# Strassen rounds of the last projection: weight sums by accumulating transfers, activation sums in two parts

## What is computed

```python
def _mla_layer(x, qpos, kn, kr, v, kpos, g_norm, w_in, g_qa, w_uq, g_qn, g_qr, w_out):
    ...
    o = _sweep_queries(_mla_block, (qn, qr), qpos, (kn, kr, v, kpos))
    o = o.reshape(B, T, MLA_WIDTH) * jax.nn.silu(gate)
    return x + o @ w_out
```

## Time and profile before

| | |
|---|---|
| median of 3 runs | 2152.32 us (2151.77 to 2152.51) |
| the profiled execution | 2152.91 us, its span 2151.1 us |
| PE | 2140.8 us busy |
| DVE | 1206.8 us busy |
| ACT | 985.7 us busy |
| POOL | 247.8 us busy |
| DMA | 225.31 MB in the span, mean 105 GB/s |
| granted PE clock | 1.0 of full speed |

### The profile page before, as it was taken

The page is one execution under the profiler, slowest core; times in us unless marked ns, Lnnn a source line. Parts: engine busy times, 40 slices in busy tenths (PEclk is TensorE's granted clock), DMA queues, the critical chain, the costliest instruction groups (busy, mean ns, idle before and its releaser), DMA issues.

```text
span 2151.1 us, 33839 instructions
## 1 busy us (share of the span) xinstructions
PE 2140.8 (100%) x11705; PEld 1881.4 (87%) x11705; DVE 1206.8 (56%) x2777; ACT 985.7 (46%) x2287; POOL 247.8 (12%) x261
## 2 busy tenths in 40 slices
PE   9999999999999999999999999999999999999999
PEld 7888888888888888888888988888899999998899
DVE  6645554445554455556223344444467777775986
ACT  5544444434444444444223333443366666665432
POOL 1000000000000000000000000421342001022011
PEclk9999999999999999999999999999999999999999
DMA  5333333333233333333442332343332212223351
GB/s 185 107 104 108 107 102 92 114 108 95 89 112 105 104 104 104 96 115 103 144 143 76 118 103 89 126 134 123 129 103 81 58 49 64 57 60 101 140 173 63
DMA packets 127463, 225.31 MB, mean 105 GB/s; under 512 B 21104, under 2 KB 75120, under 8 KB 127264
## 3 DMA queue, kind: packets, MB, share of 16 engines
q1 hardware_dynamic: 127392, 224.36, 32.9%
HBM read 191.42 MB, written 32.89 MB: 104 GB/s over the span
## 4 chain that ended last, share of the span: by engine, by line
PE 94%; DVE 3%; ACT 1%; issue 1%; DMA 1%; POOL 0%; SPq 0%; DVEq 0%; ACTq 0%; POOLq 0%
PE bank L212 66%; PE bank L2649 8%; PE bank L2001 4%; PE bank L84 1%; PE bank L958 1%; PE bank L934 1%; PE bank L2706 1%; PE bank L2684 1%; PE bank L950 1%; PE bank L2700 1%; PE bank L2686 1%; PE bank L1994 1%; PE bank L926 1%; PE bank L2678 1%; DVE h_tlo L1879 0%
## 5 line engine op out<-in xcount | busy, mean ns | idle before, releaser
L212 PE MATMUL bank<-b_whi,x_hi 128*128 128x512 f32 x1016 | 401.2, 395 | 0.6 <-DVE b_wlo L195 0.6
L212 PE MATMUL bank<-b_whi,x_lo 128*128 128x512 f32 x1016 | 396.8, 391 | 0.0
L212 PE MATMUL bank<-b_wlo,x_hi 128*128 128x512 f32 x1016 | 396.7, 390 | 0.0
L195 DVE SCALAR_TENSOR_TENSOR b_wlo<-b_raw,first,b_whi 128x512 fp32r<-128x512 f32 x254 | 179.2, 746 | 141.3 <-ACT b_whi L182 140.7
L182 ACT ACTIVATE b_whi<-b_raw,first 128x512 fp32r<-128x512 f32 x254 | 169.2, 714 | 158.1 <-PE bank L212 133.1
L212 PEld LDWEIGHTS bank<-b_whi,x_lo 128*128 128x128 f32 x1016 | 190.7, 188 | 40.7
L212 PEld LDWEIGHTS bank<-b_whi,x_hi 128*128 128x128 f32 x1016 | 191.0, 188 | 37.0 <-DVE b_wlo L195 1.3
L212 PEld LDWEIGHTS bank<-b_wlo,x_hi 128*128 128x128 f32 x1016 | 191.0, 188 | 35.4
L212 PE MATMUL bank<-m_whi,x_hi 128*128 128x512 f32 x320 | 125.0, 391 | 0.0
L212 PE MATMUL bank<-m_wlo,x_hi 128*128 128x512 f32 x320 | 124.6, 389 | 0.0
L212 PE MATMUL bank<-m_whi,x_lo 128*128 128x512 f32 x320 | 124.6, 389 | 0.0
(11 more groups left out here) (549 smaller groups left out, 5377.0 us busy)
## 6 DMA issues: line engine op xcount, KB each, us to landing
b_raw<-w_fox SPq DMA_DIRECT2D x127, 512.0 KB, 3.5
m_raw<-w_mla SPq DMA_DIRECT2D x40, 512.0 KB, 3.5
c_raw<-w_out SPq DMA_DIRECT2D x32, 512.0 KB, 3.5
h_ring<-w_out2s SPq DMA_DIRECT2D x16, 768.0 KB, 6.2
f_raw<-w_ukv SPq DMA_DIRECT2D x16, 512.0 KB, 3.6
queries<-e_q SPq DMA_DIRECT2D x16, 480.0 KB, 3.9
e_raw<-w_uq SPq DMA_DIRECT2D x32, 192.0 KB, 2.6
f_qa<-queries SPq DMA_DIRECT2D x16, 320.0 KB, 3.6
```

The lines of the kernel that those rows point to most:

```text
L195: op = eng.scalar_tensor_tensor(lo[:, k, :], raw[:, k, :], self.gain[:, K:K + 1], hi32[:, k, :], ALU.mult, ALU.subtract)
L212: op = eng.matmul(out, a, w[:, k, :], start=(first and k == 0 and i == 0), stop=(last and k == self.kk - 1 and i == len(pairs) - 1))
```

## The change

The weight sums are no longer made by DVE. POOL issues transfers that add a block in memory onto the block in the ring (`accum_op=ALU.add`), by halves (`grow`): B11 + B12 for P5, + B22 for P6, + B21 for P4, all in the slot of B11, and B22 + B12 for P7. Only B11, B22 and B21 are loaded plainly. As only additions are made, signs change in the activation sums, in `take`, in `join` and in the sample rows. `hi` waits for `grown` once for each half. The activation sums are made for seven of the eight units at the pairs (4, 4), (5, 1), (5, 3), (5, 4), and for the eighth at (7, 0).

```diff
--- before.py
+++ after.py
@@ -1665,11 +1665,13 @@
 
     N, ROUNDS, UNITS, SLOTS = 384, 2, 4, 4
     ORDER = ["P1", "P5", "P6", "P3", "P7", "P2", "P4"]
-    ROLE = {"P1": 0, "P5": 0, "P6": 0, "P3": 2, "P7": 1, "P2": 2, "P4": 0}
-    FORMED = {"P5": 0, "P6": 1, "P7": 2, "P4": 3}
-    FORM_AFTER = {"P1": 0, "P5": 1, "P6": 2, "P2": 3}
+    ROLE = {"P1": 0, "P5": 0, "P6": 0, "P4": 0, "P3": 1, "P7": 1, "P2": 2}
+    LOADED = (0, 2, 3)
+    GROWN = {"P5": (0, 1, "P1"), "P6": (0, 2, "P5"), "P7": (1, 1, "P3"), "P4": (0, 3, "P6")}
     PAIRS = ((5, 6), (1, 2), (3, 4))
     ADDS = {"P1": ((0, 0),), "P5": ((1, 1), (0, 1)), "P6": (None,), "P3": ((0, 1),), "P7": (None,), "P2": ((0, 0),),
             "P4": ((1, 0),)}
@@ -1689,7 +1691,8 @@
         self.shi, self.ring, self.thi, self.tlo, self.R, self.tmp, self.resid, self.out = sums_hi, ring, thi, tlo, R, tmp, resid, out
         s, n = c.sem, len(self.ORDER)
         self.in_ = [[s(f"h_in{i}{h}", 1, 16) for h in range(2)] for i in range(3)]
-        self.t_hi, self.t_lo, self.formed = s("h_t_hi", 4 * n), s("h_t_lo", 4 * n), s("h_formed", 16)
+        self.t_hi, self.t_lo = s("h_t_hi", 4 * n), s("h_t_lo", 4 * n)
+        self.grown = [[s(f"h_grown{i}{h}", (3, 1)[i], 16) for h in range(2)] for i in range(2)]
         self.used, self.done = s("h_used", 3 * n), s("h_done", 2 * n)
         self.summed, self.s_hi, self.s_lo = s("h_summed"), s("h_s_hi"), s("h_s_lo")
         self.taken = s("h_taken", 2 * sum(len(a) for a in self.ADDS.values()))
@@ -1722,16 +1725,15 @@
         return self.ring[self.slot(r, self.ROLE[p])][:, 2 * u:2 * u + 2, :]
     def arrived(self, eng, r, role, u):
-        n = {0: 0, 1: 1, 2: 2, 3: 2}[role]
-        i = self.slot(r, n)
-        loads = [(q, role_) for q in range(self.ROUNDS) for role_ in range(4) if self.slot(q, min(role_, 2)) == i]
+        i = self.slot(r, role)
+        loads = [(q, x) for q in range(self.ROUNDS) for x in range(3) if self.slot(q, x) == i]
         self.in_[i][u // 2].wait(eng, 0, loads.index((r, role)) + 1)
     def load(self, sp, r, role, h):
-        i = self.slot(r, min(role, 2))
-        sp.dma_start(self.ring[i][:, 4 * h:4 * h + 4, :], self.w[r, role, h]).then_inc(self.in_[i][h].sem, 16)
+        i = self.slot(r, role)
+        sp.dma_start(self.ring[i][:, 4 * h:4 * h + 4, :], self.w[r, self.LOADED[role], h]).then_inc(self.in_[i][h].sem, 16)
     PIECES = [(0, 0), (1, 1), (0, 1), (1, 0)]
     READY = {(0, 0): "P2", (1, 1): "P7", (0, 1): "P3", (1, 0): "P4"}
@@ -1762,10 +1764,6 @@
             self.load_res(sp, 0, i)
         for r in range(self.ROUNDS):
             more = r + 1 < self.ROUNDS
-            for h in range(2):
-                self.formed.wait(sp, r, 8 + 2 * h + 2)
-                self.wait_split(sp, r, "P3", 2 * h + 1)
-                self.load(sp, r, 3, h)
             self.wait_taken(sp, r, "P3")
             self.store(sp, r, 2)
             if more:
@@ -1778,7 +1776,6 @@
             self.store(sp, r, 5)
             if more:
                 for h in range(2):
-                    self.formed.wait(sp, r, 12 + 2 * h + 2)
                     self.wait_split(sp, r, "P2", 2 * h + 1)
                     self.load(sp, r + 1, 1, h)
             self.wait_taken(sp, r, "P2")
@@ -1805,45 +1802,48 @@
 
-    def form(self, pool, r, j, u):
-        k = slice(2 * u, 2 * u + 2)
-        a, b, c = (self.ring[self.slot(r, i)][:, k, :] for i in range(3))
-        p, dst, x, y, role = (("P1", a, b, a, 1), ("P5", a, c, a, 2), (None, b, c, b, None), ("P6", a, c, a, 3))[j]
-        if p:
-            self.wait_split(pool, r, p, u)
-        if j == 2:
-            self.formed.wait(pool, r, u + 1)
-        if role is not None:
-            self.arrived(pool, r, role, u)
-        pool.tensor_tensor(dst, x, y, ALU.subtract).then_inc(self.formed.sem, 1)
+    def grow(self, pool, r, p):
+        role, k, before = self.GROWN[p]
+        block = {"P5": 1, "P6": 2, "P7": 1, "P4": 3}[p]
+        x = self.ring[self.slot(r, role)]
+        for h in range(2):
+            self.wait_split(pool, r, before, 2 * h + 1)
+            pool.dma_start(x[:, 4 * h:4 * h + 4, :], self.w[r, block, h], accum_op=ALU.add).then_inc(self.grown[role][h].sem, 16)
     def join(self, pool, r, p):
         self.wait_taken(pool, r, p)
         for a, n in {"P6": ((0, 1),), "P7": ((1, 1), (1, 0))}[p]:
             self.wait_res(pool, r, (a, n))
             x = self.R[:, 2 * a:2 * a + 2, n * self.N:(n + 1) * self.N]
-            pool.tensor_tensor(x, x, self.both[:], ALU.add).then_inc(self.joined.sem, 1)
+            pool.tensor_tensor(x, x, self.both[:], ALU.subtract if n else ALU.add).then_inc(self.joined.sem, 1)
     def pool(self, pool):
         for r in range(self.ROUNDS):
+            for p in ("P5", "P6", "P7"):
+                self.grow(pool, r, p)
             self.join(pool, r, "P6")
+            self.grow(pool, r, "P4")
             self.join(pool, r, "P7")
 
-    def add_up(self, eng, i):
-        a11, a12, a21, a22 = (self.view(self.o, k, q) for q in range(2) for k in range(2))
-        dst, x, y, op = ((a22, a21, a22, ALU.add), (a21, a11, a21, ALU.subtract), (a11, a22, a11, ALU.subtract),
-                         (a12, a12, a11, ALU.subtract))[i]
+    def add_up(self, dve, i, part):
+        a11, a12, a21, a22 = (self.view(self.o, k, q)[:, part, :] for q in range(2) for k in range(2))
+        n = (0 if part.start == 0 else 4) + i
         if i:
-            self.summed.wait(eng, 0, i)
-        eng.tensor_tensor(dst, x, y, op).then_inc(self.summed.sem, 1)
+            self.summed.wait(dve, 0, n)
+        if i < 2:
+            op = dve.tensor_tensor(*((a22, a22, a21, ALU.subtract) if i == 0 else (a21, a11, a21, ALU.subtract)))
+        else:
+            x, y = (a11, a22) if i == 2 else (a12, a11)
+            op = dve.scalar_tensor_tensor(x, y if i == 2 else x, -1.0, x if i == 2 else y, ALU.mult, ALU.subtract)
+        op.then_inc(self.summed.sem, 1)
     SPLIT_SUMS = ["P5", "P6", "P3", "P7"]
     def sum_hi(self, act_, p):
         if p == "P5":
-            self.summed.wait(act_, 0, 4)
+            self.summed.wait(act_, 0, 8)
         if p == "P3":
             self.home.wait(act_, 0, 2)
         act_.activation(self.shi[p], self.view(self.o, *self.SUM_AT[p]), ACT.Copy).then_inc(self.s_hi.sem, 1)
@@ -1867,10 +1867,11 @@
                 self.done.wait(eng, r, 2 * j + 2)
     def hi(self, act_, r, p, u):
-        if p in self.FORMED:
-            self.formed.wait(act_, r, 4 * self.FORMED[p] + u + 1)
+        if u % 2 == 0 and p in self.GROWN:
+            role, k, _ = self.GROWN[p]
+            self.grown[role][u // 2].wait(act_, r, k)
         elif u % 2 == 0:
-            self.arrived(act_, r, 3 if p == "P2" else self.ROLE[p], u)
+            self.arrived(act_, r, self.ROLE[p], u)
         self.before(act_, r, p, u)
         act_.activation(self.thi[u][:], self.source(r, p, u), ACT.Copy).then_inc(self.t_hi.sem, 1)
 
@@ -1924,7 +1925,7 @@
                     self.wait_res(dve, r, at)
                     x = self.R[:, 2 * at[0] + m, at[1] * self.N:(at[1] + 1) * self.N]
                 y = self.both[:, m, :] if p == "P1" else self.bank(r, p, m)[:, 0:self.N]
-                dve.tensor_tensor(x, x, y, ALU.add).then_inc(self.taken.sem, 1)
+                dve.tensor_tensor(x, x, y, ALU.subtract if at and at[1] else ALU.add).then_inc(self.taken.sem, 1)
         if p in self.NEWS:
             i = self.NEWS.index(p)
             self.moved.wait(dve, r, self.MOVES[p])
@@ -1934,7 +1935,7 @@
             for n in self.NEW_TO[p]:
                 self.wait_res(dve, r, (0, 0))
                 x = self.R[0:NEW, SM, n * self.N:(n + 1) * self.N]
-                dve.tensor_tensor(x, x, self.tmp[:], ALU.add).then_inc(self.new_added.sem, 1)
+                dve.tensor_tensor(x, x, self.tmp[:], ALU.subtract if p == "P1" and n else ALU.add).then_inc(self.new_added.sem, 1)
     def dve(self, dve, early):
         for r in range(self.ROUNDS):
@@ -1942,8 +1943,6 @@
                 for u in range(self.UNITS):
                     if r or j or u >= early:
                         self.lo(dve, r, p, u)
-                    if p in self.FORM_AFTER:
-                        self.form(dve, r, self.FORM_AFTER[p], u)
                     if r == 0 and u == 3 and j < len(self.SPLIT_SUMS):
                         self.sum_lo(dve, self.SPLIT_SUMS[j])
                     if u == 2 and (j or r):
@@ -2917,7 +2916,7 @@
     assert S.queries_at + TT * 2 * Fast.N * 4 <= S.late_at and S.f_base + 24576 + Fast.N * 4 <= S.gate_at
     EARLY = 2
     G2, U = proj.G, KT // UK
-    SUMS_AT = {(U - 2, 4): 0, (U - 1, 0): 1, (U - 1, 1): 2, (U - 1, 3): 3}
+    SUMS_AT = {(U - 4, 4): 0, (U - 3, 1): 1, (U - 3, 3): 2, (U - 3, 4): 3}
     started = lambda g: not isinstance(g, int) or g > 0
     LAST_TWO = (HEADS // 2 - 2, HEADS // 2 - 1)
 
@@ -3095,9 +3094,12 @@
                     if (u, t) == (U - 2, 2):
                         G2.make_lo(dve, 0, U - 1)
```

(9 more changed lines are left out.)

## The result

| | before | after |
|---|---|---|
| median | 2152.27 us (2151.77 to 2152.87) | 2158.86 us (2157.45 to 2159.69) |
| span of the profiled execution | 2151.1 us | 2157.3 us |
| P1 starts | 2003.70 | 2003.92 |
| P3 starts | 2039.78 | 2042.90 |
| last matmul starts | 2147.90 | 2154.09 |

The ratio is 1.0029 (95% interval 1.002 to 1.0037): the change makes the kernel slower by 6.6 us, where I had forecast 2.9 us less. It is the other sign. DVE did get its relief (1175.4 us busy, 1206.8 before), and it bought nothing.

What follows compares the result with a forecast made beforehand. PE bounds the kernel, waiting on DVE's `lo` before P3. P3 at 2020.65 + L1 + L2 (9.5 + 6.7) = 2036.85 gains 2.9 us: 2152.3 - 2.9 = 2149.4, own case 2148 to 2156, whole range 2146.5 to 2160.

Steps and rivals of the forecast that it cites:

- The ceiling: PE's waits before P3 of round 0: without them P3 starts at 2034.2 instead of 2039.78, at most 5.6 us, 0.26%.
- The sums in two parts: Activation sums before P1: seven eighths made early, P1's `lo` of units 2 and 3 sooner, its 1.30 us wait gone.
- L2: Issue to landing of the second half of P6's adding transfer, with DMA engines idle: 6.7 us.
- L1: Issue to landing of the second half of P5's adding transfer, beside output and residual traffic: about 9.5 us, bounds 5.5 and 15.
- The failed step: DVE's `take` of P1, ahead of `lo` of P5's unit 3, put at 2.45 us, 2021.25 to 2023.70.
- T + 5.15: End of `lo` of P5's unit 3, 5.15 us after P5's second half lands at T; P6's second half is issued there.
- The last sentence of the prediction: Called the prediction wrong if landings exceed 9 us, slowed loads make `take` wait for residuals, or the queue costs time at start or end.
- The rest of the rounds: Products after P3's start in round 0: transfers cost nothing at 6.7 us landing; from 7.8 on, round 1 pays too.
- S(P5) + 4.9: Round 1: P6's second half issued 4.9 us after P5's start, behind ACT's copies, `take` and `lo`.
- Rival 2: POOL's transfers take over 9 us each, by software-written descriptors or the add: 2159.6 us; chance 0.17.
- Rival 1: Destination's read is hidden, transfers land in about 4.4 to 5.5 us: the whole 5.6 us gained, 2146.7; chance 0.30.
- Rival 3: POOL must wait for a DVE gap to prepare each transfer, 4 us at two issues: 2158.1 us; chance 0.11.

Runs made afterwards that it cites:

- experiment 7: Kernel before, with only the activation sums in two parts at the places of the change, weight sums still by `form` on DVE: 2150.30 us, ratio 0.9992.
- experiment 8: Changed kernel with its activation sums in one part at the old places, so the transfers alone: 2159.97 us, ratio 1.0036.
- Experiment 3: Changed kernel with `take` of P1 and ACT's bank copies behind `lo` of P5's unit 3, both rounds; residual loads left in place: 2151.47 us, ratio 0.9997.
- Experiment 5: Changed kernel with all sixteen POOL transfers as plain loads that overwrite the block, weight sums left out: 2148.53 us, ratio 0.9981.
- 9: Kernel before, with activation sums in two parts and P7's four `form` instructions behind P3's units instead of P6's, both rounds: 2147.92 us, ratio 0.9978.
- 10: Kernel before, with only P7's four `form` instructions moved behind P3's units instead of P6's, in both rounds: 2149.95 us, ratio 0.999.

## Why the prediction was wrong, point by point

- *The ceiling (5.6 us, P3 at 2034.2)*: it stands, though no kernel reached it. P1 to P3 is 30.5 us by it, and the best kernel needs 31.36; that kernel's 2147.92 stands 1.2 above the 2146.7 of the text.
- *The sums in two parts*: the result was right (P1's `lo` of units 2 and 3 ended at 2007.9, for 2007.7; the 1.30 us wait gone; worth 1.7 us alone). One piece was off and cost nothing: the last two long sums took 6.42 us together, against 4.16 for the first two. The three-operand form is not the reason: experiment 7 makes the same two sums with two operands, and they take 6.42 us as well; in experiment 8 a three-operand one of 128x2048 takes 2.29 us, like the others. The two slow ones run beside POOL's split of unit 7, whose two instructions grow there from 2.85 us together (2.40 and 0.45) to 5.0. I had left out that sums and split, moved beside one another, slow each other.
- *L2 = 6.7*: right, 6.7. *L1 = 9.5*: 10.2, off by 0.7. Their sum, 16.9 instead of 16.2, would have left a gain of 2.2 us. The two unknown prices were not where it went wrong.
- **The failed step is `take` of P1, which the chain has at its 2.45 us of work, with no wait for its data.** The chain had lo(P5, unit 3) at T + 5.15. With T = 2018.4 that is 2023.6; it ended at 2028.1, because `take` waited 4.41 us for `h_R`. P6's second half went out 6.1 us later than put (2028.45 for 2022.35), of which this wait is 4.4, L1 0.7, the issue of P5's half 0.5, and POOL's start behind the `lo` 0.4. I charged the full stretch of 2009 to 2012 to the transfer that runs into it (L1), and not to the loads that were already in it, though it is the same time on the same 16 engines. Two transfers of 4.5 us on all 16 engines came into it, 9 us in all, and by the table by stretch of the changed kernel the engines are full until 2024, where before their share was 0.03 in 2017 to 2018 and 0.00 in 2021 to 2024:

```profile
2012.00:2016.00 4.00, 4.00 (x25) 4.00 (x24) 0.05 (x1) 0.00 (x0) 0.87 (x1) 1.00 0.97 182
2016.00:2020.00 4.00, 4.00 (x25) 4.00 (x24) 0.70 (x1) 1.55 (x3) 0.00 (x0) 1.00 1.05 252
2020.00:2024.00 4.00, 3.53 (x21) 3.21 (x19) 0.26 (x1) 3.95 (x6) 0.00 (x0) 1.00 0.92 242
```

The last load that `take` of P1 needs, the 96 KB of sample rows, is the fourth of five that SP issues in 6.65 us from 2007.17; at the 5 us of before it would have been there by 2018, and `take` wanted it at 2020.3. Experiment 3 shows what the step was worth: with `take` behind that `lo` the kernel takes 7.4 us less, 5.8 us of it ahead of P3. The last sentence of the prediction named this failure and gave it no price and no chance.
- *The rest of the rounds*: I had the issue of P6's second half in round 1 at S(P5) + 4.9. P5 starts at 2093.55 and the issue comes at 2101.10, + 7.55: P5's own second half landed 10.6 us after 2084.87, so `hi` of unit 2 starts only at 2095.49, and behind it the same order again (`lo`, `take`, `lo`) takes up 4.3 us. From 2101.10: 7.5 landing, 1.8 for `hi` and `lo`, and PE goes on at 2110.52 after 1.55 us. P6 of round 1 takes 2.5 us longer than before, P7 of round 0 0.6. From P3's start on the kernel loses 3.1 us in all, where I had put nothing at my landing times. (The 7.8 us given for P6's half were too few: 11.1 + 4.2 - 4.9 - 1.8 leaves 8.6. At 7.5 us both cost nothing; what failed is the 4.9.)
- *Rival 2 (slow transfers, 2159.6)* gave the nearest time, for a partly wrong reason: queue and add alone make 6.7 us, and over 9 only comes with other traffic. *Rival 1 (the destination's read is hidden)* falls: 6.7 against 4.7, and twice the engine time. *Rival 3 (POOL waits for a gap of DVE)*: no row shows it. At 2008.20 DVE is 0.18 us into a low half, and the issue takes the 0.88 us that is their median.
- The Trainium skill (Collectives: The Full Stack, on the bandwidth ceiling) says that an add takes two source reads and halves the rate. Experiment 5 agrees in the engines' time, 3.2% against 1.7%. The 5.5 us estimated from its figure was too low for a lone transfer, which took 6.7. The Trainium skill (DMA: Bandwidth & Descriptors, Anatomy of one DMA) fits a transfer from GpSimd's queue as 2.0 us and the bytes at 436 GB/s, 3.8 us for a half (an estimate). The plain one took 4.7 us alone in experiment 5, so the measurement decides against that figure.

What stays open: how the rest of the rounds splits among the adding kernels (108.6 to 111.4 in one profiled execution each, with runs that spread over 2.2 to 3.5 us where POOL issues transfers, adding or plain, against 1.3 to 1.7 us in experiments 7, 9 and 10). The cheapest remedies were not tried: both loads of the sample rows issued ahead of the other residual loads, and `take` of P5 behind `lo` of P3's unit 0. Nor were finer pieces (a transfer for each unit) or a `form` for P5 alone beside transfers for the others, which would need a fourth ring slot.

## What to carry to other kernels

When work goes from a compute engine to DMA, add up the DMA engines' time of the stretch it goes into and give the longer landing to every transfer in it, not only to the new one; then look who waits for the old ones. Before a wait is put on a new producer, walk the queue in front of the instruction that releases it: here one `take` in front of one `lo` was worth 7 us. Look at what is counted, too: the wait was for 96 KB of sample rows, fourth in SP's line. And before work is given to another engine, try the order: moving four instructions of each round on DVE gave 2.2 us alone and 4.0 with the sums in two parts, more than the sixteen adding transfers gave in any arrangement that was run. A wait that the trace puts down to a busy engine may need only an instruction of that engine placed elsewhere.

## What the runs showed of the hardware

- An accumulating transfer of 768 KB from POOL's queue landed in 6.7 to 6.8 us with the engines otherwise idle and in 6.8 to 7.1 with some of SP's traffic left, a plain one in 4.7; it held the 16 engines for 4.5 us against 2.3. The page counts 200.86 MB read from memory in both, so the destination, which lies in the ring on the chip, costs engine time and no memory traffic.
- Beside one another in a full stretch, two accumulating transfers took 10.5 us and loads of 384 KB 12.8 us (7.4 and 7.7 us with plain transfers in the same place).
- Moving the residual loads ahead of the store only swapped them: the 384 KB loads of round 0 from 12.7 us to 5.7, the 1 MB store from 5.0 to 15.1.
- An issue took POOL 0.88 us with the add and 0.54 without. The one at 2008.20 took 0.88 us with DVE inside a two-input instruction.
- DVE's sums and POOL's split, both of which read the tile `o_mla`, slowed each other where they ran at once: DVE's two sums from 4.16 to 6.42 us, POOL's two instructions from 2.85 to 5.0.
- After 4.6 us without a matmul the granted clock was 0.50 (1.2 GHz) for the next 5 us; here it cost nothing, because PE was not what the next product waited for.
